# Suffix sums of stick-breaking attention: exact float32 matmuls before, two matmul passes over a rounded part and a remainder after

## The reference

```python
z = jnp.einsum('bhqd,bshd->bhqs', qb, kf)
q_pos = blk * Q_BLOCK + jnp.arange(Q_BLOCK)
strict = key_pos[None, :] < q_pos[:, None]
log_keep = jnp.where(strict, jax.nn.log_sigmoid(-z), 0.0)
log_after = lax.cumsum(log_keep, axis=3, reverse=True) - log_keep
w = jnp.where(strict, jnp.exp(jax.nn.log_sigmoid(z) + log_after), 0.0)
```

## Time and profile before

| | value |
|---|---|
| median of 3 runs | 1221.74 us |
| the profiled execution, its own time | 1221.35 us |
| span of its trace | 1219.4 us |
| PE busy | 1213.9 us, 9146 matmul records |
| DVE, ACT, POOL busy | 927.2, 682.0, 349.0 us |
| mean granted TensorE clock | 0.999 of full speed |

### The profile page before, as it was taken

The page is one execution under the profiler, slowest core; times in us unless marked ns, Lnnn a source line. Parts: engine busy times, 40 slices in busy tenths (PEclk is TensorE's granted clock), DMA queues, the critical chain, the costliest instruction groups (busy, mean ns, idle before and its releaser), DMA issues.

```text
span 1219.4 us, 23522 instructions
## 1 busy us (share of the span) xinstructions
PE 1213.9 (100%) x9146; PEld 1144.8 (94%) x9146; DVE 927.2 (76%) x1170; ACT 682.0 (56%) x1025; POOL 349.0 (29%) x496
## 2 busy tenths in 40 slices
PE   9999999999999999999999999999999999999998
PEld 8999989999999999999999999999999999999998
DVE  6867788998687876666777778789997787766665
ACT  6666646673654564545566656557637445544552
POOL 0088991340304200000001889905303051000000
PEclk9999999999999999999999999999999999999999
DMA  8654554444345565455445454454443456545441
GB/s 311 242 207 157 187 175 171 173 173 139 104 174 177 203 252 209 171 186 190 174 162 217 173 206 169 175 180 167 166 142 110 172 188 227 208 172 206 172 172 69
DMA packets 32322, 220.36 MB, mean 181 GB/s; under 512 B 3712, under 2 KB 4352, under 8 KB 6272
## 3 DMA queue, kind: packets, MB, share of 16 engines
q1 hardware_dynamic: 31824, 218.91, 50.1%
q10 hardware_dynamic: 432, 0.52, 0.1%
HBM read 218.37 MB, written 1.05 MB: 180 GB/s over the span
## 4 chain that ended last, share of the span: by engine, by line
PE 99%; DMA 0%; DVE 0%; SPq 0%; ACT 0%; issue 0%
PE banks L567 22%; PE banks L522 20%; PE banks L524 20%; PE banks L523 20%; PE banks L569 11%; PE banks L535 4%; DMA hT<-x_t 0%; PE banks L781 0%; PE banks L829 0%; DVE s5u L1811 0%; ACT u_t L976 0%; DVE u_t L1327 0%; DVE rstd_row L1411 0%; SPq L466 0%; DVE w_lo_t L1336 0%; DVE hT L1521 0%
## 5 line engine op out<-in xcount | busy, mean ns | idle before, releaser
L1282 DVE TENSOR_TENSOR w_lo_t<-raw,w_hi_t 128x1024 fp32r<-128x1024 f32 x394 | 493.5, 1292 | 94.3 <-ACT w_hi_t L946 93.8
L946 ACT ACTIVATE w_hi_t<-raw 128x1024 fp32r<-128x1024 f32 x394 | 393.5, 1046 | 133.1 <-PE banks L524 129.1
L522 PE MATMUL banks<-u_t,w_hi_t 128*128 128x256 f32 x928 | 266.1, 287 | 0.6 <-DVE w_lo_t L1336 0.5
L524 PE MATMUL banks<-u_t,w_lo_t 128*128 128x256 f32 x928 | 263.2, 284 | 0.0
L523 PE MATMUL banks<-u_t,w_hi_t 128*128 128x256 f32 x928 | 263.2, 284 | 0.0
L567 PE MATMUL banks<-b_t,w_hi_t 128*128 128x512 f32 x576 | 204.0, 398 | 0.0
L567 PE MATMUL banks<-u_t,w_hi_t 128*128 128x512 f32 x576 | 204.0, 398 | 0.0
L522 PE MATMUL banks<-h_hi_t,w_hi_t 128*128 128x256 f32 x672 | 190.2, 283 | 0.0
L523 PE MATMUL banks<-h_lo_t,w_hi_t 128*128 128x256 f32 x672 | 190.2, 283 | 0.0
L524 PE MATMUL banks<-h_hi_t,w_lo_t 128*128 128x256 f32 x672 | 190.1, 283 | 0.0
L522 PEld LDWEIGHTS banks<-u_t,w_hi_t 128*128 128x128 f32 x928 | 178.7, 193 | 4.6 <-issue 4.2
(11 more groups left out here) (273 smaller groups left out, 1976.7 us busy)
## 6 DMA issues: line engine op xcount, KB each, us to landing
raw<-weights SPq DMA_DIRECT2D x201, 1024.0 KB, 4.8
raw<-weights SPq DMA_DIRECT2D x3, 512.0 KB, 8.2
prm<-params SPq DMA_DIRECT2D x1, 1250.5 KB, 5.9
prm<-params SPq DMA_DIRECT2D x1, 1238.5 KB, 9.9
raw<-weights SPq DMA_DIRECT2D x4, 256.0 KB, 6.7
out_t<-hT SPq DMA_DIRECT2D x4, 256.0 KB, 2.2
cst<-constants SPq DMA_DIRECT2D x1, 704.0 KB, 9.9
hT<-x_t SPq DMA_DIRECT2D x1, 512.0 KB, 7.1
```

The source lines that it names most:

```text
L522: pe.matmul(o, st[0], mv[0], start=start, stop=False, skip_group_check=True)
L524: ins = pe.matmul(o, st[1], mv[0], start=False, stop=stop, skip_group_check=True)
L946: act.activation(w_hi[:, slot, a:a + HALF], raw[:, slot, a:a + HALF], ACT.Copy) \
L1282: dve.tensor_tensor(w_lo[:, slot, a:a + HALF], raw[:, slot, a:a + HALF], w_hi[:, slot, a:a + HALF].bitcast(F32), ALU.subtract) \
```

## The change

The soft-plus in `attA` is split like the weights: ScalarE writes its rounded part `sp_hi` (fp32r) in its steps 6 and 7, VectorE writes the remainder `sp_lo = attA - sp_hi` in its steps 7 and 8. ScalarE also copies the two constant matrices into fp32r (`tri`) in its step 5. Per head, TensorE now runs the three matmuls twice, once over `sp_hi` and once over `sp_lo`, all in the dense format. They stand behind block 9 and no longer behind block 8. The exponential on ScalarE goes from step 8 to step 9, and the clipping on VectorE from step 9 to step 10. The new tiles lie in `b_t`, which is free at that time. Two semaphores, `sb_hi` and `sb_lo`, are added, each counting twice in a layer. The line numbers of the changed kernel are higher by 7 in TensorE's helpers, by 9 to 16 further down and by 21 behind VectorE's pieces.

```diff
@@ -299,6 +301,9 @@
         st_early = attB[:, :, :].rearrange("p h c -> p (h c)")[:, 0:4 * T].rearrange("p (a b t) -> p a b t", a=2, b=2)
         st_late = G[:, 1, 4:8, :].rearrange("p (a b) t -> p a b t", a=2)
         st_of = [st_early, st, st_late, st]
+        sp_hi, sp_lo = (b_t[:, n, 0:6, :].rearrange("p k t -> p (k t)").rearrange("p (h c) -> p h c", h=HEADS)
+                        for n in range(2))
+        tri = b_t[:, 0, 6, :].rearrange("p (a q) -> p a q", a=2)
         squares = [U[:, 2 * q:2 * q + 2, :] for q in range(4)]
         ab, hf = sbqk, yb[:, :, 0, :]
 
...
@@ -744,12 +751,14 @@
 
                     def sb_suffix(h):
 
-                        pe.wait_ge(s.sb_sp, layer * PER.sb_sp + h // 2 + 1)
-                        bank = SB_BANK[h]
-                        single(banks[:, bank, 0:T], c("neg_suffix"), attA[:, h, 0:T], False, False)
-                        single(banks[:, bank, P:T], c("neg_ones"), attA[:, h, T:ATT], False, False)
-                        single(banks[:, bank, T:ATT], c("neg_suffix"), attA[:, h, T:ATT], False, True) \
-                            .then_inc(s.sb_acc, 1)
+                        pe.wait_ge(s.sb_lo, layer * PER.sb_lo + h // 2 + 1)
+                        bank = banks[:, SB_BANK[h], :]
+                        for part in (sp_hi, sp_lo):
+                            last = part is sp_lo
+                            single(bank[:, 0:T], tri[:, 0, :], part[:, h, 0:T], False, False)
+                            single(bank[:, P:T], tri[:, 1, :], part[:, h, T:ATT], False, False)
+                            ins = single(bank[:, T:ATT], tri[:, 0, :], part[:, h, T:ATT], False, last)
+                        ins.then_inc(s.sb_acc, 1)
 
                     def gla_scores():
 
@@ -802,7 +811,7 @@
                             for tt in range(2):
                                 ins = single(banks[:, 2 + tt, ATT:512], p_("w_gate"), gq[:, tt * P:(tt + 1) * P], False)
                             ins.then_inc(s.gla_z, 1)
-                        if m == 8:
+                        if m == 9:
                             for h in range(HEADS):
                                 sb_suffix(h)
                         if m == 11:
@@ -1154,7 +1163,14 @@
                         for h in (0, 2):
                             act.activation(attA[:, h:h + 2, :], attA[:, h:h + 2, :], ACT.Ln, bias=one_c) \
                                 .then_inc(s.sb_ln, 1)
-                    if m == 8:
+                    if m == 5:
+                        act.activation(tri[:, 0, :], c("neg_suffix"), ACT.Copy)
+                        act.activation(tri[:, 1, :], c("neg_ones"), ACT.Copy)
+                    if m in (6, 7):
+                        h = 2 * m - 12
+                        act.wait_ge(s.sb_sp, layer * PER.sb_sp + m - 5)
+                        act.activation(sp_hi[:, h:h + 2, :], attA[:, h:h + 2, :], ACT.Copy).then_inc(s.sb_hi, 1)
+                    if m == 9:
                         for h in (0, 2):
                             act.wait_ge(s.sb_acc, layer * PER.sb_acc + h + 2)
                             act.activation(attA[:, h:h + 2, :], scored(h), ACT.Exp).then_inc(s.sb_exp, 1)
@@ -1674,7 +1690,12 @@
                         own.link(dve.scalar_tensor_tensor(out=two, in0=banks[:, SB_BANK[h]:SB_BANK[h] + 2, 0:ATT],
                                                           scalar=0.0, in1=two, op0=ALU.max, op1=ALU.add))
                         dve.tensor_tensor(diagonal(two), diagonal(two), strict, ALU.mult).then_inc(s.sb_sp, 1)
-                    if m == 9:
+                    if m in (7, 8):
+                        h = 2 * m - 14
+                        dve.wait_ge(s.sb_hi, layer * PER.sb_hi + m - 6)
+                        dve.tensor_tensor(sp_lo[:, h:h + 2, :], attA[:, h:h + 2, :], sp_hi[:, h:h + 2, :].bitcast(F32),
+                                          ALU.subtract).then_inc(s.sb_lo, 1)
+                    if m == 10:
                         for h in range(HEADS):
                             one = attA[:, h, :].rearrange("p (c q) -> p c q", q=P)[:, 0:3:2, :]
                             dve.wait_ge(s.sb_exp, layer * PER.sb_exp + h // 2 + 1)
```

More of the change, by code:

```diff
@@ L168 @@
     sb_sp = 2
+    sb_hi = 2
+    sb_lo = 2
     sb_acc = HEADS
@@ L388, in build @@
         s.sb_sp = sem("sb_sp")
+        s.sb_hi = sem("sb_hi")
+        s.sb_lo = sem("sb_lo")
         s.sb_acc = sem("sb_acc")
```

## The result

| | before | after |
|---|---|---|
| median | 1221.55 us (4 runs) | 1233.36 us (4 runs, 1231.83 to 1233.76) |
| ratio | | 1.0102, interval 1.0089 to 1.0114 |
| profiled execution | 1221.35 us | 1233.66 us |
| mean granted clock | 0.999 (profiled execution) | 0.993 to 0.996 (4 runs) |

The ratio is the one on record; the quotient of the two medians is 1.0097. The change makes the kernel 1.0% slower, some 12 us. The forecast was 1230.2 us, 8.5 over before: right in direction and in its main mechanism, short by 3.2 us, with the measured time at the very end of its range.

What follows compares the result with a forecast made beforehand. TensorE, busy for 1213.9 of 1219.4 us, was taken as the bound. Profiled 1221.35 us, plus 7.4 for two layers (each -3.5 old burst, +2.7 new, +4.5 waiting), plus 1.45 for one clock drop, gave 1230.2; range 1227.0 to 1233.4.

Steps and rivals of the forecast that it cites:

- The waits behind block 9: TensorE's suffix matmuls wait for VectorE's remainders: 0.4 us for heads 0 and 1, 4.1 us for heads 2 and 3.
- ScalarE's slip: In step 6 ScalarE waits 1.8 us for the masked soft-plus; all that follows on it moves by 2.6 us.
- The narrow dense matmuls: Dense 128-column matmuls in the new burst were priced at 0.107 us each, making 0.67 us a head.
- the rival of a slow narrow form: Dense 128-column suffix matmuls cost 0.214 us as in plain float32, 0.86 us more a layer: 1231.9 us; chance 0.17.
- Attend level with the maskings: Behind block 11, maskings end at 280.4 and attend wants them at 280.5: priced at nothing, up to 0.3 us a layer.
- The 0.8 us a layer that the shorter burst gains without any wait: Suffix burst of four heads: old 3.5 us less new 2.7 us per layer, if TensorE never waits.
- The rival "VectorE is in time": Remainders of heads 2 and 3 finish by 263.0, so nothing waits behind block 9: 1219.7 us; chance 0.05.
- The clock: TensorE's clock drops to 1.2 GHz at one of the two new waits: 1.45 us, bounds 0 and 2.9.
- The rival of two drops: Both new waits drop TensorE's clock, one more drop of 1.45 us: 1231.7 us; chance 0.18.
- The range: Whole kernel: 1227.0 us, with no drop and less waiting, to 1233.4 us, with two drops and slow narrow matmuls.

Runs made afterwards that it cites:

- e4: Changed kernel with 36 filler matmuls of 128 columns between heads 1 and 2, filling TensorE's wait; 1228.49 us, ratio 1.0053.
- e2: Changed kernel without the remainder subtractions on VectorE, TensorE streaming the rounded part twice; 1223.49 us, ratio 1.0018.
- e9: Kernel of e6 with addition and scan of S5 pair 2 moved from VectorE's step 8 to the end of step 9; 1220.08 us, ratio 0.9990.
- e3: Changed kernel with ScalarE's first rounding moved behind the sixteen exponentials in step 6; 1229.93 us, ratio 1.0070.
- e8: Kernel of e4 with 18 filler matmuls in place of 36, half of the wait filled; 1231.74 us, ratio 1.0092.
- e7: Kernel of e5 with ScalarE's first rounding behind the sixteen exponentials as in e3; 1230.57 us, ratio 1.0071.
- e5: Changed kernel with both remainder subtractions in VectorE's step 7, directly behind its weights; 1228.49 us, ratio 1.0053.
- e1: Kernel before with only the place changed: plain float32 suffix matmuls behind block 9, exponentials and maskings one step later; 1220.40 us, ratio 0.9997.
- e6: Kernel of e7 with the maskings back in VectorE's step 9, ahead of the linear attention products; 1220.67 us, ratio 0.9996.
- e10: Kernel of e2 with the maskings back in VectorE's step 9; 1220.62 us, ratio 0.9994.

## Why the prediction was right in direction and short in size

- *The waits behind block 9.* Right in cause and nearly in size. The second remainder was forecast for 267.5 and ended at 267.19. The first was ready at 261.78 instead of 262.1, so heads 0 and 1 did not wait (0.4 us forecast). The weights of step 7 took 2.55 us to the next instruction, not 2.84, because GpSimd had finished earlier: it ran mostly alone while VectorE idled. So there were two waits, 7.6 us in all, and not "some 9 us in four waits". Per layer 3.35 us were lost at full clock where 3.7 were forecast; e4, in which the clock never falls, loses 3.5 us a layer in this stretch.
- *ScalarE's slip.* Right: 1.83 us of waiting, 2.66 us of delay; block 9 starts at 256.03, 0.1 us later, behind the evacuation of sbv. e2 shows that without any remainder on VectorE this would have brought 1.8 us of waiting a layer at attend.
- *The narrow dense matmuls.* Right: e2 has 2.68 us for four heads, 0.67 for one; the rival of a slow narrow form is excluded.
- *Attend level with the maskings.* Right for the changed kernel (they end at 282.29; attend starts at 282.4). The 0.8 us a layer that the shorter burst gains without any wait show only in e9. As the change is written they were out of reach: e2 removes the first wait and finds the second. The rival "VectorE is in time" took the first wait for the only one.
- *The clock.* This is the step that failed. "I expect such a drop at one of the two new waits: 1.45 us, bounds 0 and 2.9." It came at both, and one is not worth 1.45 us. The trace gives 2.3 us in layer 0 and 3.2 in layer 1, 5.5 in all; the comparison of e4 with the changed kernel gives 4.9. The size was taken from the earlier trace rows, where TensorE was at work before the drop and after it, and it was held fixed. There the clock was low for 3.4 us; behind the two waits of 3.8 us it was low for 6.9. It covers the remaining half of the burst, 2.62 us instead of 1.31, and the first part of block 10. The rival of two drops had the right case and the wrong price: 1231.7, where 1221.35 + 7.4 + 5.5 = 1234.3 would have been the sum. With the waits as they were, 1221.35 + 6.7 + 5.5 = 1233.55, and the profiled execution took 1233.66. The clock was 4.0 us too small and the waits 0.7 too large, so a part of the error cancelled.
- *The range.* That its upper end, 1233.4, still reaches the median of 1233.36 is luck. It contains 1.7 us for slow narrow matmuls, which did not occur; two drops at the price of the prediction end at 1231.7.
- *Two slips without weight.* The earlier trace rows lists four waits in three lines, not three. And 5.83 - 5.76 is 0.07 us, not 0.09.

What stays open: when the clock falls, and what sets the length of a low stretch. An empty 3.8 us was followed by 6.9 us of low clock in both layers. An empty 3.0 us (e3) and an empty 1.8 us (e8) behind block 9 were followed by 3.4 us. An empty 1.8 us ahead of attend (e2) was followed by none, and an empty 2.3 us there by the low clock at once in e7 and only behind gla_scores in e5. The small matmuls behind block 11 bring it in some executions and not in others. What came before the waits differs, but no run varies that alone.

## What to carry to other kernels

Where one engine is busy for the whole span, a shorter piece of its work is worth its length only if every operand comes earlier too: replay the other engines' written order up to each wait, the second and third as well as the first, because a wait hides the ones behind it. An empty stretch of TensorE can cost more than its length, since what follows may run at the lower clock. In this kernel 1.8 to 3.8 us of waiting behind block 9 drew another 1.7 to 3.2 us in a layer, while 1.8 us ahead of attend drew nothing. The price is half of that part of the low stretch in which TensorE has work. An instruction that waits at the head of a long queue (here 0.85 us of rounding ahead of a table load and sixteen exponentials) belongs behind whatever is ready; e3 shows 3.4 us for it in the changed kernel.

## What the runs showed of the hardware

- The runs of the unchanged kernel lie in steps. In the batch with e9, fourteen of 21 take 1219.76 to 1220.61 us at a mean clock of 1.000, five 1221.66 to 1222.03 at 0.998 or 0.999, and two 1223.14 and 1223.56 at 0.997. The steps of 1.5 us fit the 1.45 us that the drop behind gla_scores costs in the earlier trace rows, none, one or two times in an execution. The kept traces agree: e1 and e6 have none, the kernel before has one, e9 and e10 have two. The median moves with their count.
- Filler matmuls over the whole wait kept the clock up in all four executions of e4, and the time fell by 4.9 us; over half of it they did not (e8). The Trainium skill ("TensorE: Matmul & The Clock Gate", section "HAM oscillation — how this bites in real kernels") warns of the half-rate clock after waits between bursts; the traces agree for the waits of 1.8 to 3.8 us behind block 9. The waits of 1.8 us ahead of attend in e2, with a granted clock of 1.00 behind them, and those of 0.64 us in e6 brought none.
- VectorE's subtraction of 2 x 1024 columns took 2.35 us with GpSimd idle, 2.63 to 3.49 with GpSimd at work in part or all of it; GpSimd's own additions took 0.74 us alone and 1.6 beside it.
